# Up projections of the experts loaded through ScalarE's DMA queue in a two-block layer on one core

## The reference

```python
def run_block(args):
    xb, e = args
    return (jax.nn.silu(xb @ w_gate[e]) * (xb @ w_up[e])) @ w_down[e]
# w_gate, w_up: (32, 1024, 512); w_down: (32, 512, 1024), float32
```

## Time and profile before

| what | value |
|---|---|
| median of 3 runs | 1060.18 us (1056.91 to 1061.52) |
| span of the profiled execution, first to last instruction | 1058.3 us |
| PE busy | 76% of the span |
| ACT busy | 32% |
| traffic | 287.05 MB, nearly all read from HBM |
| expert stage, from the end of the first expert's matmuls (L1901) to the last landing of a down matrix that TensorE waits for | about 264 to 719 us |

### The profile page before, as it was taken

One profiled execution on the slowest core, in us unless ns is written; L12 is line 12 of the kernel. 1 busy time (PEld: TensorE's weight loads), 2 busy tenths in 40 slices (PEclk: granted clock), 3 DMA queues, 4 the chain that ended last, 5 costly groups with the idle time before them and its releaser, 6 DMA issues.

```text
span 1058.3 us, 16170 instructions
## 1 busy us (share of the span) xinstructions
PE 805.9 (76%) x6846; PEld 633.8 (60%) x6846; DVE 430.0 (41%) x722; ACT 333.8 (32%) x552; POOL 75.5 (7%) x100
## 2 busy tenths in 40 slices
PE   5999999985655566655657447476798979999996
PEld 4979998765332243322424225243697779999995
DVE  4854858545130021301203012031757665455555
ACT  4754355630101101001011010011576454444443
POOL 1018425000000000000000000000100000000000
PEclk9999999986888688777889677798899999999998
DMA  5994424466999999999999999999944436456101
GB/s 202 282 367 160 142 101 158 159 244 253 365 399 396 395 375 397 398 398 394 375 400 396 399 397 358 399 398 363 331 152 159 159 123 206 169 179 214 46 1 40
DMA packets 139239, 287.05 MB, mean 271 GB/s; under 512 B 11369, under 2 KB 34206, under 8 KB 139166
## 3 DMA queue, kind: packets, MB, share of 16 engines
q1 hardware_dynamic: 138834, 285.37, 73.6%
q10 hardware_dynamic: 332, 0.58, 0.2%
HBM read 284.90 MB, written 1.05 MB: 270 GB/s over the span
## 4 chain that ended last, share of the span: by engine, by line
PE 38%; issue 23%; SPq 21%; DMA 10%; DVE 3%; ACT 3%; POOL 1%; ACTq 0%; POOLq 0%; DVEq 0%
SPq L684 15%; PE bank L547 13%; DMA down_b<-in_w_down_dram 9%; SPq L689 6%; PE bank L581 5%; PE bank L1901 4%; PE bank L1916 3%; PE bank L1886 3%; PE bank L559 3%; PE bank L1929 2%; DMA ring<-in_w_in_dram 1%; ACT w_hi L522 1%; PE bank L1732 1%; PE bank L1745 1%; DVE w_lo L532 1%
## 5 line engine op out<-in xcount | busy, mean ns | idle before, releaser
L547 PE MATMUL bank<-act_p,w_hi 128*128 128x256 f32 x1440 | 269.9, 289 | 9.7 <-issue 5.8
L532 DVE TENSOR_TENSOR w_lo<-ring,w_hi 128x1024 fp32r<-128x1024 f32 x138 | 179.2, 1299 | 157.0 <-ACT w_hi L522 156.8
L547 PEld LDWEIGHTS bank<-act_p,w_hi 128*128 128x128 f32 x1440 | 229.1, 196 | 13.7 <-issue 9.0
L522 ACT ACTIVATE w_hi<-ring 128x1024 fp32r<-128x1024 f32 x138 | 145.9, 1058 | 195.6 <-PE bank L547 136.7
L547 PE MATMUL bank<-act_p,w_lo 128*128 128x256 f32 x720 | 206.4, 287 | 0.0
L547 PEld LDWEIGHTS bank<-act_p,w_lo 128*128 128x128 f32 x720 | 140.7, 195 | 0.0
L1517 DVE COPY y_e<-bank 32x256 f32<-32x256 f32 x64 | 27.2, 424 | 235.9 <-PE bank L1916 235.5
L1916 PE MATMUL bank<-down_b,h_t 128*32 128x256 f32 x512 | 49.2, 551 | 81.8 <-DMA down_b<-in_w_down_dram 80.0
L581 PE MATMUL bank<-w_hi,act_q 128*128 128x512 f32 x304 | 95.3, 394 | 0.4 <-issue 0.4
L1040 ACT ACTIVATE y_e<-bank 32x256 f32<-32x256 f32 x64 | 23.9, 374 | 213.5 <-PE bank L1916 213.1
L1901 PE MATMUL bank<-ring,x_t 128*32 128x256 f32 x1536 | 89.9, 387 | 0.0
(11 more groups left out here) (332 smaller groups left out, 889.0 us busy)
## 6 DMA issues: line engine op xcount, KB each, us to landing
ring<-in_w_up_dram SPq DMA_DIRECT2D x24, 2048.0 KB, 22.0
ring<-in_w_gate_dram SPq DMA_DIRECT2D x24, 2048.0 KB, 18.8
ring<-in_w_in_dram SPq DMA_DIRECT2D x16, 2048.0 KB, 18.7
down_b<-in_w_down_dram SPq DMA_DIRECT2D x16, 2048.0 KB, 19.3
down_a<-in_w_down_dram SPq DMA_DIRECT2D x16, 2048.0 KB, 19.3
ring<-in_w_ffn_in_dram SPq DMA_DIRECT2D x22, 1024.0 KB, 6.6
pair_d<-in_w_gate_dram SPq DMA_DIRECT2D x8, 2048.0 KB, 19.1
pair_d<-in_w_up_dram SPq DMA_DIRECT2D x8, 2048.0 KB, 22.0
```

The source lines that it names most:

```text
L522: nc.scalar.activation(parts(w_hi, g, view), view, ACT.Copy).then_inc(split_hi, 1)
L532: nc.vector.tensor_tensor(parts(w_lo, g, view), view, h, ALU.subtract).then_inc(split_lo, 1)
L547: mm = nc.tensor.matmul(dst, parts(wt, g, grans[g][1])[:, k, :], a[:, x_part, k, :], start=(k == 0 and i == 0), stop=(k == KC - 1 and i == 2))
```

## The change

Loads of gate and down stay where they were, on SyncE. In the expert loop, up of expert e+4 is no longer issued by SyncE but by ScalarE, in `expert_act` of expert e, between the silu (L1035) and the wait for the transposed product. The destination, the source and the semaphore that counts the landing are the same. The up loads of experts 0 to 3 and those of any further rounds stay on SyncE. ScalarE's loop is split for this: seven turns of four experts with a load, four experts without one, and further rounds under a condition.

```diff
+    def half_of(eng, i, n, e):
+
+        eng.dma_start(PAIR[i][:, n, :].rearrange("p (k n) -> p k n", k=KC),
+                      w[("w_gate", "w_up")[n]][e].rearrange("(k p) n -> p k n", p=P))\
+           .then_inc(landed_pair[n] if i == 3 else landed[PAIR_SLOT[i] + n], 16)
...
-        def load_expert(i, used, e, e_down):
+        def load_expert(i, used, e, e_down, halves):
 
             sp.wait_ge(gu_raw, used)
-            load_half(i, 0, e)
-            load_half(i, 1, e)
+            for n in halves:
+                load_half(i, n, e)
             sp.wait_ge(ye_raw, used)
             load_down(i, e_down)
...
         with sp.Fori(1, NE // 4) as j:
             for i in range(4):
-                load_expert(i, 4 * j + i - 3, 4 * j + i, 4 * j + i - 2)
+                load_expert(i, 4 * j + i - 3, 4 * j + i, 4 * j + i - 2, (0,))
...
-        def expert_act(x, e):
+        def expert_act(x, e, up_next=None):
             act.wait_ge(gu_raw, x + 1)
             nc.scalar.activation(h_e[:, :], bank[0][:, 0:P], ACT.Silu).then_inc(gate_silu, 1)
+            if up_next is not None:
+                half_of(act, e, 1, up_next)
             act.wait_ge(ht_raw, x + 1)
...
-        with act.Fori(0, n_rounds) as r:
-            with act.Fori(0, NE // 4) as k:
-                for e in range(4):
-                    expert_act(NE * r + 4 * k + e, e)
+        with act.Fori(0, NE // 4 - 1) as k:
+            for e in range(4):
+                expert_act(4 * k + e, e, 4 * k + 4 + e)
+        for e in range(4):
+            expert_act(NE - 4 + e, e)
+        with act.If(n_rounds > 1):
+            with act.Fori(1, n_rounds) as r:
+                with act.Fori(0, NE // 4) as k:
+                    for e in range(4):
+                        expert_act(NE * r + 4 * k + e, e)
```

More of the change, by code:

```diff
@@ L682, in load_half @@
         def load_half(i, n, e):
-            sp.dma_start(PAIR[i][:, n, :].rearrange("p (k n) -> p k n", k=KC),
-                         w[("w_gate", "w_up")[n]][e].rearrange("(k p) n -> p k n", p=P))\
-              .then_inc(landed_pair[n] if i == 3 else landed[PAIR_SLOT[i] + n], 16)
+            half_of(sp, i, n, e)
         def load_down(i, e):
@@ L720, in _ @@
                 for i in range(4):
-                    load_expert(i, NE * r + i - 3, i, (i - 2) % NE)
+                    load_expert(i, NE * r + i - 3, i, (i - 2) % NE, (0, 1))
                 with sp.Fori(1, NE // 4) as j:
                     for i in range(4):
-                        load_expert(i, NE * r + 4 * j + i - 3, 4 * j + i, 4 * j + i - 2)
+                        load_expert(i, NE * r + 4 * j + i - 3, 4 * j + i, 4 * j + i - 2, (0, 1))
         before_third = sp.value_load(rounds_i[0:1, 1:2], min_val=NE - 3, max_val=NE * T // CAP - 3)
```

## The result

The changed kernel takes 1080.66 us (median of 4, 1079.16 to 1083.28) against 1060.51 for the kernel before (4 runs): ratio 1.0189, interval 1.0163 to 1.0215, so 20 us slower. The profiled execution has a span of 1077.4 us, 19.1 more than before.

A forecast was written before the change was run, and what follows sets the result against it. It took the chip's DMA, with its queue full, as the bound of the expert stage. Three jumps at 8.3 us gave +25, all other terms 0, so 1060.2 + 25 = 1085 us, range 1054 to 1100.

The forecast's parts named there:

- holes at the three jumps: TensorE's loop jumps in the expert stage: DMA queues run empty, 8.0 us of hole each; 1085 us, chance 0.62.
- The bound: Expert stage: the full DMA queue bounds it at 390 GB/s; removing SyncE's 28 up issues is worth 0.
- ScalarE's issues: 28 issues between silu and copy, 0.38 us each, hidden behind TensorE's wait for down: 0, up to +10 allowed.
- The sharing: Two full queues take equal turns, up gets half of the traffic and lands about 12.9 us after its issue.
- The cover: Bytes queued when down lands before a jump: 23.3 us where it was 31.6, so 8.3 us less.
- The sum: Lost DMA time at the three jumps is not regained: 3 x 8.3 = 25 us.
- The group ends: Group ends inside the loop body: pause 21.2 us under 23.3 of cover, cost 0, 2.1 us to spare.
- Hidden anyway: Rival: sharing keeps need's order, or issue waits at the jump go with SyncE's long issues; 1060 us, chance 0.20.
- Faster by rate: Rival: two queues let the DMA engines overlap rows; 1034 us at 414 GB/s, 1046 half way, chance 0.12.
- Much slower by longer fetches: Rival: instruction fetches, or the copy behind ScalarE's issue, wait behind both queues; 1111 us, chance 0.06.
- up's landing near 20 us: Sign that the forecast is wrong, order kept; if right, up lands 11 to 14 us after issue instead of 22.0.
- waits for down as before: Sign that the forecast is right: TensorE's waits for down matrices, 80.0 + 43.8 us, stay unchanged.

The follow-up runs named there:

- the twenty-two loads: Changed kernel, but the up loads of experts 10, 11, 18, 19, 26 and 27 stay on SyncE, loops written out: 1059.80 us, ratio 0.9996 to the kernel before.
- the kernel with six moved: Kernel before with only the up loads of experts 10, 11, 18, 19, 26, 27 on ScalarE, loops written out: 1090.15 us, ratio 1.0287.
- the written-out kernel: Changed kernel with TensorE's expert loop written out, so no jump stands between groups: 1059.83 us, ratio 0.9989 to the kernel before.
- the order in the one queue: Kernel before, all on SyncE, with down issued ahead of gate and up from expert 8 on: 1054.88 us, ratio 0.9960.
- a loop written out: Kernel before with TensorE's expert loop written out: 1054.83 us, ratio 0.9953.

## Why the prediction was right

It said 1085, 1054 to 1100, slower with a chance of 0.69; measured 1080.7. The mechanism, holes at the three jumps, is the one that the runs show; two steps on the way to its size were off, and that they hardly show in the sum is in part luck.

*The bound.* Right: a full DMA queue at the same 397 GB/s in both kernels. That removing SyncE's long issues is worth 0 is borne out by the twenty-two loads that cost and gave nothing. So the Trainium skill's rule (DMA: Bandwidth & Descriptors, Issuing engines are not separate DMA queues) holds as far as it goes, that issuing elsewhere brings no bandwidth; it doesn't speak of the order in which bytes arrive, and here that was the 20 us.

*ScalarE's issues.* 0.38 to 0.49 us each, and the copy as soon as before behind its transposed product: 0, as taken.

*The sharing.* This step was off in its form. I took half of the traffic for up at all times and a landing after 11 to 14 us; it landed after 22.0. The trace's records of DMA packets, counted per queue by the time of their start from the span's first instruction, show why:

```
time, us     SyncE's queue, packets 2 KB / 4 KB   ScalarE's, 2 KB   GB/s SyncE / ScalarE
482 to 485     0 / 200                            205               273 / 140
501 to 504    32 / 168                            214               251 / 146
508 to 511   283 / 0                              283               193 / 193
518 to 522   624 / 77                               0               398 /   0
```

Where both have work they are served in nearly equal numbers of packets: 283 and 283, 200 and 205. Beside gate's rows of 2 KB up gets half of the bytes, beside down's rows of 4 KB a third. That is more than up needs on average, but by less than I took, and an up load also waits behind the one before it. With the queue otherwise empty it still starts late: its first packet comes 3.6 to 3.8 us after the issue in the six loads of the kernel with six moved, where I had taken 1.2. So the Trainium skill's rule of turns by packets (same page, Queues, rings and completion order) agrees with the trace's counts for these two queues; my reading of it as half of the bytes didn't.

*The cover.* I worked out 8.39 MB on SyncE's side and 0.86 MB of up left when the down lands; the packet records give 7.88 and 0.99, 8.87 MB or 22.3 us. (My 23.3 us ran to the last landing, and so 22.1 to the last byte.) The 0.99 is luck: three errors cancel. The load of up was issued 10.6 us ahead of that landing (496.46, 507.07) and not 7.4, since TensorE waited longer for down; its bytes came from about 3.6 us after the issue on and not 1.2; and they flowed at some 160 GB/s, not at 199.

*The sum.* 3 x 8.3 = 25 is the term that was mis-sized: measured 20.9, 7.0 at each jump. The hole itself was nearly right, 8.0 worked out and 26.5 / 3 = 8.8 measured. What was too large is the cover of the kernel before. By my 12.58 MB, 31.6 us, against 28.9 + 2.4 there should have been no dip at all, and yet I had read one there. The packet records give 11.8 MB or 29.7 us left at 492.62, so the change took 29.7 - 22.3 = 7.4 us of cover and not 8.3. The dips of before were 1.8 us each by all their windows, not 1.2, and are part of the base: 8.8 - 1.8 = 7.0. Hole less dip with my own numbers, 3 x (8.0 - 1.2), would have given 20.4.

*The group ends.* 0 was right for the changed kernel, none of its windows there is under 370 GB/s. The margin is thinner than I had it, as the written-out kernel shows.

*The rivals.* "Hidden anyway" by shorter issue waits at the jump: they went from 24.9 us to 22.5, as the changed kernel's waits say,

```profile
PE bank L1898 <- issue: 22.5, 6, 4.5
```

so next to nothing of them is due to SyncE's long issues. Faster by rate: 397.3 against 397.4, no. Much slower by longer fetches: no. The prediction's list of signs had up's landing near 20 us as a sign that the order of need was kept; that sign was badly chosen, since a load can land late after its issue and still early against its need. It also had "waits for down as before", and they grew by 19.3 us: lost DMA time has to turn up somewhere, and TensorE meets it there.

What stays open: the "issue" waits at the jump in detail. That they hang on the jump is shown, as they vanish with it. That they are instruction fetch, which I had only argued, the packet records support: the queue of kind "instruction" (q8) moves one packet of 16 KB just ahead of the end of each of the six waits, in the kernel before and in the changed one, and the matmuls go on 1.2 to 1.7 us after that packet is done (502.9 to 503.9 us ahead of 505.58, 508.6 to 509.7 ahead of 510.91). Such packets come elsewhere too, without a wait behind them. The records don't say which engine's instructions a packet holds, and why the wait takes 3 to 5 us stays open. The margin at group ends, which failed at two of them in the changed kernel written out, is open too.

## What to carry to other kernels

When one queue with a fixed order feeds an engine at the DMA's full rate, its order is a resource: the bytes still queued are what covers the next pause of the consumer. A second queue brings no rate and lets one stream run ahead into buffers that can't use it, so move only a stream with few buffers, or none. Before moving a load, find the longest pause between freed buffers, and compare it with the bytes that are still under way at its start; the cheaper mend here was the order in the one queue (with the old order kept for the first four loads), or a loop written out, each worth 0.4 to 0.5% here.

## What the runs showed of the hardware that I had not expected

Two queues full at once share by packets and not by bytes: 283 packets of 2 KB on each side give 193 GB/s each, while 200 of 4 KB against 205 of 2 KB give 273 and 140. So the length of a row sets the share of its queue. ScalarE isn't held back by SyncE's full queue: while SyncE's down issues in the full queue took 5.6 to 11.4 us in the changed kernel, ScalarE's stayed at 0.38 to 0.49 us. (No run fills ScalarE's own queue, so what it would do then isn't shown.) But a quick issue isn't a quick start: with ScalarE's queue empty and SyncE's full, the first packet came 3.6 to 3.8 us after the issue in the kernel with six moved.
